# S5 output products of a hybrid decoder trunk: four banks filled side by side instead of one after another

## The reference

```
bu_re = jnp.einsum('blgh,gph->lbgp', uf, bb_re)
bu_im = jnp.einsum('blgh,gph->lbgp', uf, bb_im)
...
_, _, xr, xi = lax.associative_scan(combine, (a_re, a_im, bu_re, bu_im), axis=0)
y = (jnp.einsum('lbgp,ghp->blgh', xr, c_re.astype(f32))
     - jnp.einsum('lbgp,ghp->blgh', xi, c_im.astype(f32))
     + d_skip.astype(f32).reshape(S5_GROUPS, S5_GROUP) * uf)
y = jax.nn.gelu(y.reshape(bsz, seq, S5_WIDTH))
y = y * jax.nn.sigmoid(y @ glu_w.astype(f32) + glu_b.astype(f32))
```

## Time and profile before

| | |
|---|---|
| median of 3 runs | 1504.6 us (1504.05 to 1516.5) |
| the profiled execution, its own time | 1505.42 us |
| its span, first to last instruction | 1503.8 us |
| PE busy | 1391.6 us (93%) |
| PE weight loads busy | 1167.0 us (78%) |
| DVE / ACT / POOL busy | 755.6 / 497.2 / 205.1 us |
| mean granted clock of TensorE | 0.929 |

### The profile page before, as it was taken

One profiled execution on the slowest core, in us unless ns is written; L12 is line 12 of the kernel. 1 busy time (PEld: TensorE's weight loads), 2 busy tenths in 40 slices (PEclk: granted clock), 3 DMA queues, 4 the chain that ended last, 5 costly groups with the idle time before them and its releaser, 6 DMA issues.

```text
span 1503.8 us, 17711 instructions
## 1 busy us (share of the span) xinstructions
PE 1391.6 (93%) x6940; PEld 1167.0 (78%) x6940; DVE 755.6 (50%) x760; ACT 497.2 (33%) x574; POOL 205.1 (14%) x250
## 2 busy tenths in 40 slices
PE   2468998999998999999999999999959999999997
PEld 2347787899886888888888788887748888888886
DVE  7693785715766566234665524433555333332343
ACT  3225342215233323122322326645533222122332
POOL 5892992500000000000000000000000000000000
PEclk7568998669998999999999799999979999999999
DMA  9216754231114577244663222121033332334232
GB/s 323 66 43 103 204 181 140 85 76 37 57 29 140 154 237 237 66 116 112 209 206 88 84 85 84 37 69 64 29 84 84 96 92 84 99 104 112 63 88 74
DMA packets 201572, 163.14 MB, mean 108 GB/s; under 512 B 25454, under 2 KB 191563, under 8 KB 199467
## 3 DMA queue, kind: packets, MB, share of 16 engines
q1 hardware_dynamic: 198288, 136.24, 31.7%
q0 software_dynamic: 2720, 25.99, 4.8%
q10 hardware_dynamic: 506, 0.12, 0.0%
HBM read 157.21 MB, written 4.19 MB: 107 GB/s over the span
## 4 chain that ended last, share of the span: by engine, by line
PE 84%; DVE 7%; ACT 3%; POOL 2%; DMA 2%; issue 1%; SPq 1%; ACTq 0%; DVEq 0%
PE banks L469 22%; PE banks L470 22%; PE banks L471 22%; PE banks L688 5%; DVE hn_lo L1579 1%; DMA ada_in<-in_ada_w_dram 1%; PE banks L720 1%; PE banks L718 1%; PE banks L945 1%; PE banks L972 1%; PE banks L544 1%; DVE ada_acc L1529 1%; PE banks L722 1%; PE banks L685 1%; ACT whi L1125 1%
## 5 line engine op out<-in xcount | busy, mean ns | idle before, releaser
L469 PE MATMUL banks<-hn_hi,whi 128*128 128x512 f32 x992 | 391.9, 395 | 6.3 <-DVE hn_lo L1579 4.9
L470 PE MATMUL banks<-hn_lo,whi 128*128 128x512 f32 x992 | 389.8, 393 | 0.0
L471 PE MATMUL banks<-hn_hi,wlo 128*128 128x512 f32 x992 | 389.2, 392 | 0.0
L1547 DVE TENSOR_TENSOR wlo<-raw,whi 128x2048 fp32r<-128x2048 f32 (+3 forms) x107 | 234.0, 2188 | 134.8 <-ACT whi L1125 73.8
L1131 ACT ACTIVATE whi<-raw 128x2048 fp32r<-128x2048 f32 (+1 forms) x66 | 123.1, 1865 | 317.8 <-PE banks L471 314.2
L469 PEld LDWEIGHTS banks<-hn_hi,whi 128*128 128x128 f32 x992 | 188.6, 190 | 49.2 <-issue 8.8
L471 PEld LDWEIGHTS banks<-hn_hi,wlo 128*128 128x128 f32 x992 | 188.5, 190 | 40.0
L470 PEld LDWEIGHTS banks<-hn_lo,whi 128*128 128x128 f32 x992 | 188.6, 190 | 38.8
L469 PE MATMUL banks<-ff_hi,whi 128*128 128x512 f32 x416 | 164.0, 394 | 0.0
L470 PE MATMUL banks<-ff_lo,whi 128*128 128x512 f32 x416 | 162.9, 392 | 0.0
L471 PE MATMUL banks<-ff_hi,wlo 128*128 128x512 f32 x416 | 162.8, 391 | 0.0
(11 more groups left out here) (402 smaller groups left out, 1853.3 us busy)
## 6 DMA issues: line engine op xcount, KB each, us to landing
raw<-in_ffn_w_in_dram SPq DMA_DIRECT2D x88, 512.0 KB, 4.8
ada_in<-in_ada_w_dram POOLq DMA_DIRECT2D x16, 1536.0 KB, 6.3
ada_in<-in_ada_w_dram SPq DMA_DIRECT2D x32, 512.0 KB, 4.4
raw<-in_ffn_w_out_dram SPq DMA_DIRECT2D x32, 384.0 KB, 4.1
raw<-in_sb_w_in_dram SPq DMA_DIRECT2D x24, 512.0 KB, 4.4
raw<-in_hy_w_in_dram SPq DMA_DIRECT2D x20, 512.0 KB, 5.7
raw<-in_ffn_w_out_dram SPq DMA_DIRECT2D x32, 320.0 KB, 3.6
ada_first<-in_ada_w_dram SPq DMA_DIRECT2D x4, 2048.0 KB, 18.3
```

The source lines that it names most:

```text
L469: pe.matmul(o, lh, rh, start=first, stop=False)
L470: pe.matmul(o, lh, rl, start=False, stop=False)
L471: return pe.matmul(o, ll, rh, start=False, stop=last)
L1547: TTO(wlo[s][:, 0:width], raw[s][:, 0:width], whi[s][:, 0:width].bitcast(F32), SUB)\
```

## The change

The four S5 banks are filled side by side. Before, bank 0 was filled with eight groups, each with its lag, real and imaginary product, then bank 1, and so on. Now a round takes one group of each bank: four lag products, then four real products, then four imaginary products; eight rounds fill all four banks. The banks' groups are also dealt out differently: banks 0 and 2 hold groups of parity 0, banks 1 and 3 those of parity 1 (before: banks 0 and 1 parity 0, banks 2 and 3 parity 1), so that neighbouring state products in a row of four use different halves of the array's rows. PE waits for all four banks before its first product, and the four banks are done at the end of the last round. The copy by ACT puts each bank where its groups belong.

```diff
@@ -707,21 +707,26 @@
-            for n in range(4):
-                q, b, _ = gp("y", n)
+            slots = [gp("y", n) for n in range(4)]
+            for q, _, _ in slots:
                 pe.wait_ge(drained[q % 4], q // 4)
-                par, i0 = n // 2, 8 * (n % 2)
-                rows = slice(64 * par, 64 * par + 64)
-                for r in range(8):
-                    i, g = i0 + r, 2 * (i0 + r) + par
-                    o = bank[b][:, r * NC:(r + 1) * NC]
+
+            def lanes(r):
+                for n, (_, b, _) in enumerate(slots):
+                    i, par = 8 * (n // 2) + r, n % 2
+                    yield bank[b][:, r * NC:(r + 1) * NC], slice(64 * par, 64 * par + 64), i, 2 * i + par
+
+            for r in range(8):
+                for o, rows, i, g in lanes(r):
                     pe.matmul(o, m_in[:, g, :], u_rows[:, g, :], start=True, stop=False)
-                    o = bank[b][:, r * NC + 1:(r + 1) * NC]
-                    pe.matmul(o, v_re[rows, i, 1:SC + 1, :], s_re[rows, i, 0:NC - 1],
+                for o, rows, i, g in lanes(r):
+                    pe.matmul(o[:, 1:NC], v_re[rows, i, 1:SC + 1, :], s_re[rows, i, 0:NC - 1],
                               start=False, stop=False)
-                    last = pe.matmul(o, v_im[rows, i, 1:SC + 1, :], s_im[rows, i, 0:NC - 1],
+                for o, rows, i, g in lanes(r):
+                    last = pe.matmul(o[:, 1:NC], v_im[rows, i, 1:SC + 1, :], s_im[rows, i, 0:NC - 1],
                                      start=False, stop=True)
-                last.then_inc(gdn_done, 1)
+                    if r == 7:
+                        last.then_inc(gdn_done, 1)
@@ -1269,7 +1274,7 @@
-                act.activation(u_pair[:, 8 * (n % 2):8 * (n % 2) + 8, n // 2, :],
+                act.activation(u_pair[:, 8 * (n // 2):8 * (n // 2) + 8, n % 2, :],
                                bank[b].rearrange("p (g c) -> p g c", c=NC), ACT.Copy).then_inc(drained[q % 4], 1)
```

## The result

The changed kernel took 1482.36 us in the median of four runs (1480.25 to 1483.24), the kernel before 1505.01 (four runs beside them). The ratio of the changed kernel to the one before is 0.9837, with a 95% interval of 0.9806 to 0.9868 (the quotient of the two medians is 0.985). A second series (changed_again, six runs) gave 1483.32 and 0.9833 (0.9795 to 0.987). The forecast was 1485 in a range of 1480 to 1501. The profiled execution took 1480.25 us, 25.2 less than the profiled one before. Of these, 4.8 us lie ahead of the change, where the clock was higher from the start of this execution, and aren't its doing.

What follows compares the result with a forecast made beforehand. PE bounds the kernel, running without a gap through the S5 outputs at a mostly low clock. Fewer shape changes and overlapping halves, less start and end waits, give -19.7 from the profiled 1505.4: 1485.7, stated as 1485 us, range 1480 to 1501.

Steps and rivals of the forecast that it cites:

- Part 1: S5 output stage on PE: six fewer changes of shape per four-group round, 48 in all; 0.93 us per round, low clock.
- Part 2: S5 state products: two row halves work at once, 16 passes take 1.80 us; round 3.91 us low clock, 2.07 high.
- Rival A: S5 state products: halves do not overlap, only shape changes are saved; -5.4 us, 1499 to 1500 us; chance 0.25.
- Part 3: Start of the S5 stage: PE also waits for DVE's drain of the fourth "at" bank; +1.05 us.
- Part 4: Clock in the S5 stage: falls at 275.2 us, after 4.0 us at the high level; stage ends at 298.9.
- rival B: S5 stage: clock stays high because PE is denser, then conditioning sums bound; 1481 to 1485 us; chance 0.22.
- Part 5: End of the S5 stage: first turn waits 0.85 us for ACT's copy, later copies hide; turns start 19.7 us earlier.
- Part 6: Behind the stage: nothing becomes late; DVE's last conditioning sum, ending at 299.54, is in time by 4 us.
- The cap: One-column sums behind the turns: PE waits until 299.54 for conditioning sums, limiting the gain to 19.8 to 23.5 us.
- The order in the SP queue: SP queue: last conditioning load is issued at 294.85, before the S5 outputs are drained at about 301.4.
- The slack of the GLU's input: S5 output read-back (prediction says GELU input): issued at 330.33 to 333.1, used at 347.26; both ends move together.
- Rival C: S5 state products: every alternation of halves drains the array like a shape change; +4.2 us, about 1509; chance 0.08.

Runs made afterwards that it cites:

- changed_again: The changed kernel once more without further edits, on one chip beside split_again; 1483.32 us, ratio 0.9833 to the kernel before.
- pairs_one_half: Changed kernel with two banks at a time, sixteen rounds, both banks of a pair holding groups of the same half; 1499.35 us, ratio 0.9942.
- alternate_only: Changed kernel's four banks and dealing, but each group does its lag, real and imaginary product in turn; 1510.48 us, ratio 1.0032 to the kernel before.
- pairs: Changed kernel with two banks at a time, one lower and one upper half, in sixteen rounds; 1485.92 us, ratio 0.983 to the kernel before.
- same_half: Changed kernel with groups dealt as before (banks 0, 1 lower half, banks 2, 3 upper half); 1481.81 us, ratio 0.9857 to the kernel before.
- late_sums: Changed kernel with PE's last conditioning sums behind products x2, four DVE sums behind its turn drains, two loads behind the output writes; 1477.59 us, ratio 0.9824.
- same_half_late: Changed kernel with the edits of same_half and late_sums together; 1478.56 us, ratio 0.9827 to the kernel before.
- split_sums: late_sums with PE's 16 one-column passes of conditioning part 4 back behind the turns, only part 5's 16 behind x2; 1474.04 us, ratio 0.9763.
- split_again: split_sums once more without further edits, on one chip beside changed_again; 1472.63 us, ratio 0.9751 to the kernel before.
- before_late: The kernel before with the conditioning sums moved as in late_sums, no other edit; 1506.37 us, ratio 1.0006.

## Why the prediction was right, point by point

- **Part 1, changes of shape.** Right. Rounds of 1.62 us (pairs_one_half) and 3.80 us per four groups (alternate_only) fit passes of 0.112 us and changes of 0.14 us: 12 x 0.112 + 2 x 0.14 = 1.62.
- **Part 2, the halves overlap.** Right, and shown by pairs against pairs_one_half. The round is 2.07 us at the high clock as predicted, and 3.80 at the low, where I had 3.91. My reason for it was too narrow: the halves need not alternate product by product, it is enough that the other half's product lies a few passes ahead (same_half). Rival A is refuted. By the Trainium skill's page "TensorEngine Tiling (Array Packing)", section Key Properties, tiles work independently; these runs agree for two halves of rows, with 0.27 us against 0.50 for four passes.
- **Part 3, the start.** Right: PE waits 0.88 us for the fourth drain and starts 0.84 us after that drain began, where I had 0.74 from the one to the other.
- **Part 4, the clock. This is the step that failed.** I let it fall 4 us into the stage. In the profiled execution it held to the end of the stage, and so it did in the profiles of changed_again, same_half, late_sums, same_half_late and split_sums; it fell in split_again. The stage took 16.6 us rather than 27.7. That was rival B, at 0.22 against 0.42 for the forecast, and its numbers are the measured ones: it has the stage end at 287.8, and ACT's first copy starts at 282.97 in a stage that began 4.7 us earlier than its sum has it; its range was 1481 to 1485, the median is 1482.4. I had taken from the kernel before that steady work of this kind pulls the clock down. What made it hold is open: no run took the clock by itself, the same instructions met both levels, and the passes that PE starts in a microsecond don't sort the profiles by themselves: the clock held over the 64 passes in 7.15 us of "lt" and "at", and fell in the pairs, with 12 in 1.18 us.
- **Part 5, the end.** Right: the turns start 0.74 us behind the start of ACT's first copy, where I had 0.7. The other three copies hide but for about 0.15 us, since at the high clock the turns take less time than the copies. (The prediction's three terms, 0.11, 0.60 and 0.1, add up to 0.81 and not to 0.85, which changes nothing.)
- **Part 6, what is late next.** I saw the conditioning sums as the next bound and had them in time by 4 us; with the held clock PE came 7.7 us too soon for them, as rival B has it. The cap explains why the wrong clock cost the forecast only some 3 us: the turns start 31.0 us earlier and not 19.7, but d2 only 23.2. That the sums are the bound is shown by late_sums (d2 starts 12 us earlier) together with before_late (no gain without the change). The rest of the way was free of new waits, as predicted. The order in the SP queue is not as predicted, though: ACT's copies end at 285.04, ahead of the last conditioning loads, and the writes stand behind these until 290.58. The slack of the GLU's input covered it.
- **How much of the agreement is luck.** The forecast of 1485 us lies 2.6 us from the median, but it is the sum of a low clock in the stage and no wait behind it, and neither was so. Where the clock did fall, the stage came out as the sum has it: the turns start 29.0 us after the fourth drain of "at" in split_again and 29.8 in the pairs, 29.3 by the forecast. But in the pairs the one-column products then took 6.8 us and not the 3.5 that the forecast had kept from the row of before, and d2 started 16.1 us earlier than before, not 19.7. By this the forecast was up to 4 us too low for its own case (an estimate from one profile).
- **Rival C** is refuted: neither the profile of the change nor alternate_only has a cost for changing halves.

Open is what decides the clock in this stage, and with it how the gain of 22.7 us divides between the overlap and the held clock: the stage took 16.6 us at the high clock and 27.8 at the low.

## What to carry to other kernels

When small products of different row counts follow each other, read the distance between starts and not the busy share: sort the products so that those of one shape stand together, and put those of the other half of the rows within a few passes, in another bank (no run here had both halves in one bank). Before you promise the whole gain, look for work that has been ready long ahead of its place on the engine: that is the next bound, and moving it is worth something only together with the first change. And compute such a stage at both clock levels, since the same program may meet either.

## What the runs showed of the hardware

- PE starts a product of the other half four passes ahead of its turn: in same_half the loads of the first and, by the reading above, of the third group start 0.013 us apart.
- Float32 passes of 64 rows and 128 weight columns start 0.112 us apart in one half (pairs_one_half). With two halves each half has its own stream with that step (pairs), so that two start in 0.112 us, at the full clock.
- A change between 128 and 64 rows costs 0.14 us at the full clock: worked out from the kernel before, and met by the round of 1.62 us in pairs_one_half.
- 32 one-column passes in a row at the full clock were followed by a fall in all the five profiles that have them: for 6.6 us at a granted clock of 0.55 in late_sums, and to about 0.5 in before, before_late, pairs_one_half and same_half_late. 16 in a row were followed by no fall in split_sums and split_again ("d8t" 3.8 us in both).
